# Hybrid mixer of a two-block network: decay spread from a split, block ends in one product, another order at its end

## The reference, cut to what matters

```python
dt = softplus(dt_raw + dt_bias);  a = -exp(a_log);  adt = dt * a
acs = cumsum(adt within chunks of 128)                     # per head
lmat = exp(where(tri, acs[l] - acs[s], -inf))              # decay between two tokens
y_diag = einsum((cc . bc) * lmat, xc)
states = einsum(bc, exp(acs[end] - acs), xc);  chunk_decay = exp(acs[end])
y_off = einsum(cc, prev_state, exp(acs))
y = y_diag + y_off + d_skip * xs
yg = rmsnorm(y * silu(z), over each of 2 groups of 256) * ssd_norm_w
out = concatenate([attn_out, yg]) @ w_out
```

## Time and profile before

| | |
|---|---|
| median of 3 runs | 3323.21 us (3322.04 to 3326.91) |
| the profiled execution | 3323.83 us, its span 3322.1 us |
| PE busy | 3273.5 us, 99% of the span, 15372 instructions |
| DVE, ACT, POOL busy | 55%, 35%, 2% |
| mean granted clock | 0.992 |
| first hybrid mixer, heads 3 to the output product | 2204 to 2300 us of the span |
| second hybrid mixer, the same part | 2818 to 2914 us |

### The profile page before, as it was taken

How to read it: one execution, slowest core, us unless ns; L and a number is a source line. 1 busy time by engine, 2 the same in 40 slices (tenths; PEclk the granted TensorE clock), 3 DMA queues, 4 the chain that set the end, 5 groups by cost and what they waited for, 6 DMA issues and landing times.

```text
span 3322.1 us, 37176 instructions
## 1 busy us (share of the span) xinstructions
PE 3273.5 (99%) x15372; PEld 2709.9 (82%) x15372; DVE 1818.9 (55%) x2599; ACT 1163.1 (35%) x1617; POOL 74.7 (2%) x108
## 2 busy tenths in 40 slices
PE   8999999999999999999999999999999999999999
PEld 6888876888888888887788888887788888878887
DVE  5664366666436664357566635876533368563332
ACT  5222253332233222263322223654322245442221
POOL 1000000000000000000000000100000010000000
PEclk8999999999999999999999999999999999999999
DMA  5443321344333443332244433210223222022322
GB/s 155 142 148 119 101 84 51 127 140 150 114 110 115 139 140 120 97 100 64 89 140 141 135 106 103 80 51 30 98 89 98 95 87 87 1 89 90 101 95 70
DMA packets 334238, 339.86 MB, mean 102 GB/s; under 512 B 12406, under 2 KB 329112, under 8 KB 334072
## 3 DMA queue, kind: packets, MB, share of 16 engines
q1 hardware_dynamic: 332112, 333.80, 30.9%
q0 software_dynamic: 1728, 3.62, 0.4%
q10 hardware_dynamic: 232, 0.06, 0.0%
HBM read 335.36 MB, written 2.10 MB: 102 GB/s over the span
## 4 chain that ended last, share of the span: by engine, by line
PE 90%; DVE 6%; ACT 2%; issue 1%; DMA 0%; SPq 0%; DVEq 0%; ACTq 0%
PE ps L135 88%; PE ps L138 2%; DVE ar L100 1%; DVE wl L100 1%; DVE ar L108 1%; ACT wh L95 1%; ACT ar L95 1%; DVE hl L108 0%; DVE T L108 0%; DMA raw<-in_ffn_w 0%; ACT L95 0%; ACT ch L95 0%; DVE ar L117 0%; ACT hh L95 0%; DVE T L100 0%
## 5 line engine op out<-in xcount | busy, mean ns | idle before, releaser
L135 PE MATMUL ps<-hh,wl 128*128 128x512 f32 x2760 | 1088.7, 394 | 13.9 <-DVE hl L108 9.4
L100 DVE TENSOR_TENSOR wl<-raw,wh 128x1024 fp32r<-128x1024 f32 (+2 forms) x547 | 654.0, 1197 | 774.4 <-ACT wh L95 774.0
L135 PE MATMUL ps<-hh,wh 128*128 128x512 f32 x2760 | 1076.8, 390 | 0.0
L135 PE MATMUL ps<-hl,wh 128*128 128x512 f32 x2760 | 1076.8, 390 | 0.0
L95 ACT ACTIVATE wh<-raw 128x1024 fp32r<-128x1024 f32 (+2 forms) x547 | 560.6, 1027 | 466.2 <-PE ps L135 461.3
L135 PEld LDWEIGHTS ps<-hh,wl 128*128 128x128 f32 x2760 | 520.0, 188 | 128.1 <-issue 18.6
L135 PEld LDWEIGHTS ps<-hh,wh 128*128 128x128 f32 x2760 | 519.6, 188 | 108.9
L135 PEld LDWEIGHTS ps<-hl,wh 128*128 128x128 f32 x2760 | 520.2, 188 | 104.4 <-issue 0.6
L135 PE MATMUL ps<-uh,wl 128*128 128x512 f32 x1056 | 412.0, 390 | 0.0
L135 PE MATMUL ps<-uh,wh 128*128 128x512 f32 x1056 | 411.2, 389 | 0.0
L135 PE MATMUL ps<-ul,wh 128*128 128x512 f32 x1056 | 411.1, 389 | 0.0
(11 more groups left out here) (241 smaller groups left out, 2722.3 us busy)
## 6 DMA issues: line engine op xcount, KB each, us to landing
raw<-in_ffn_w SPq DMA_DIRECT2D x120, 1024.0 KB, 5.1
raw<-in_w_ada SPq DMA_DIRECT2D x48, 1024.0 KB, 5.2
raw<-in_w_gate_up SPq DMA_DIRECT2D x44, 1024.0 KB, 5.0
raw<-in_m_w_in SPq DMA_DIRECT2D x26, 1024.0 KB, 5.6
raw<-in_w_down SPq DMA_DIRECT2D x16, 1024.0 KB, 5.2
raw<-in_ffn_w SPq DMA_DIRECT2D x16, 768.0 KB, 4.3
raw<-in_w_in SPq DMA_DIRECT2D x12, 1024.0 KB, 5.3
raw<-in_m_w_out SPq DMA_DIRECT2D x8, 1024.0 KB, 5.2
```

Source lines behind the costliest of these rows:

```text
L100: return self.issue(lambda e: e.tensor_tensor(out, a, b, op))
L135: return self.issue(lambda e: e.matmul(out, l, r, start=start, stop=stop, skip_group_check=True))
```

## The change

- `ad` (8 rows at partitions 32 to 39) is split: ACT writes `adh`, DVE `adl`, in free parts of `hl`, in the first step of `states()`. The spreads in `weigh` and the product with `X3` contract over these 8 rows, one-pass, with `adl` and then `adh`. `X3` is written as fp32r after that. POOL no longer clears `ad` and `X3`.
- DVE writes the chunk ends, masked by head, into 32 columns (`ends`); one product of 8 rows and 32 columns takes the place of the eight.
- The squares of slice 0 are added to those of slice 1 on DVE (`y01`); `frame_means(0)` is gone.
- `weigh(2)` moves into the step of `frames(1)`, and everything behind it comes one step earlier: frames 2 in head 7, frames 3 and means 2 in head 8, means 3 in head 9 and, in head 9's second slot, the wait for `v8` and `along`, ahead of `values(7)`.
- DVE forms `v8` in three operations instead of two.
- The output product of tiles 0 and 1 runs over slices 0, 4, 1, 5, 2, 6, 3, 7 in one go; ACT's and DVE's parts of attention's and of the recurrence's slices follow in turn, with DVE's `scaled` between them.

```diff
@@ -205,7 +205,8 @@
         sq = [sb(f"sq{i}", [128, S])[0] for i in range(2)]
         acc, _ = sb("acc", [128, S])
         T1 = [sb(f"T1{i}", [128, S])[0] for i in range(2)]
-        T3 = [sb(f"T3{i}", [128, S])[0] for i in range(2)]
+        X3, o_3 = sb("X3", [128, S], F32R)
+        T3 = [sb("T30", [128, S], F32, o_3)[0], sb("T31", [128, S])[0]]
         adab, _ = sb("ada", [128, 424])
         mod, _ = sb("mod", [128, 96])
...
@@ -1081,8 +1074,8 @@
                     W = [d.rearrange(tok4, b=4) for d in xd]
                     Bt = [sp[:, 8, :], sp[:, 9, :]]
                     PV = [None, sp[:, 10, :], sp[:, 11, :], sp[:, 12, :]]
-                    X3 = T3[0][:, :]
                     E2 = [T3[1][:, :], sp[:, 13, :]]
+                    adh, adl = hl[32:40, 6, :], hl[32:40, 7, :]
                     b = banks.take((s, "dtk"))
                     pe.wait_ge(worked, (s, "ad"))
                     for a, src in enumerate((sq[1], ad)):
...
@@ -1091,10 +1084,8 @@
                             done = pe.tr(b[:, c:c + 8], src[32:40, 128 * k:128 * k + 128], ident[32:40, 32:40])
                     done.then_inc(formed, (s, "dtk"))
                     b = banks.take((s, "ends"))
-                    ends = ad.rearrange("p (b n) -> p b n", n=128)[:, :, 127]
-                    for hd in range(8):
-                        done = pe.mm(b[:, 4 * hd:4 * hd + 4], ident[:, 32 + hd:33 + hd].to_broadcast([128, 128]), ends)
-                    done.then_inc(formed, (s, "ends"))
+                    pe.wait_ge(worked, (s, "ends"))
+                    pe.mm(b[:, 0:32], one[32:40, :].to_broadcast([8, 128]), sq[0][32:40, 0:32]).then_inc(formed, (s, "ends"))
 
                     def turned(t):
                         b = banks.take((s, "xt", t))
...
@@ -1113,14 +1104,20 @@
                         done.then_inc(formed, (s, "sn", c))
 
                     def weigh(t):
+                        pe.wait_ge(hi_part, (s, "ad"))
+                        pe.wait_ge(lo_part, (s, "ad"))
                         for hd in (2 * t, 2 * t + 1):
                             b = banks.take((s, "w", hd))
-                            pe.mm(b[:, :], ident[:, 32 + hd:33 + hd].to_broadcast([128, 128]), ad, True, False)
+                            row = identr[32:40, 32 + hd:33 + hd].to_broadcast([8, 128])
+                            pe.mm(b[:, :], row, adl, True, False)
+                            pe.mm(b[:, :], row, adh, False, False)
                             pe.mm(b[:, :].rearrange(tok4, b=4), above[:, :], identr[:, :].unsqueeze(1).to_broadcast([128, 4, 128]),
                                   False, True).then_inc(formed, (s, "w", hd))
                         b = banks.take((s, "e", t))
                         pe.wait_ge(worked, (s, "X3"))
-                        pe.mm(b[:, :], X3[:, 128 * t:128 * t + 128], ad).then_inc(formed, (s, "e", t))
+                        rows = X3[32:40, 128 * t:128 * t + 128]
+                        pe.mm(b[:, :], rows, adl, True, False)
+                        pe.mm(b[:, :], rows, adh, False, True).then_inc(formed, (s, "e", t))
 
                     def frames(t):
                         b = banks.take((s, "y2", t))
...
@@ -1138,7 +1135,6 @@
                         done.then_inc(formed, (s, "y", t))
 
                     def frame_means(t):
-                        pe.wait_ge(squared, (s, "y", t))
                         for k in range(4):
                             done = pe.mm(bs[:, 4 * t + k:4 * t + k + 1], E2[t % 2][:, 128 * k:128 * k + 128], ones[:, 0:1])
                         done.then_inc(formed, (s, "ys", t))
...
@@ -1166,22 +1162,23 @@
                     frames(0)
                     yield 1
                     frames(1)
-                    yield 1
+                    weigh(2)
+                    yield 1
+                    weigh(3)
                     bs = banks.take((s, "ystat"), hold=True)
-                    frame_means(0)
-                    weigh(2)
-                    yield 1
+                    pe.wait_ge(worked, (s, "y01"))
                     frame_means(1)
-                    weigh(3)
                     yield 1
                     frames(2)
                     yield 1
                     frames(3)
                     yield 1
+                    pe.wait_ge(squared, (s, "y", 2))
                     frame_means(2)
+                    yield 1
+                    pe.wait_ge(squared, (s, "y", 3))
                     frame_means(3)
                     banks.drop((s, "ystat"))
-                    yield 1
                     yield 1
                     pe.wait_ge(pooled, (s, "v8"))
                     for g in range(2):
...
@@ -1211,16 +1208,16 @@
                     between()
                     if hd > 1:
                         values(hd - 2)
+                while next(ssd, 0):
+                    pass
                 for j in range(4):
                     b = banks.take((s, "cat", j), freed=(lo_part, (s, "c", j)))
                     pe.wait_ge(*left_of((s, "val", 7)))
                     for q in range(4):
                         done = pe.tr(b[:, 128 * q:128 * q + 128], A(12 + q)[:, 128 * j:128 * j + 128], ident[:, :])
                     done.then_inc(formed, (s, "cat", j))
-                rest = begin(s, [("out", 0), ("out", 1)], ch, cl, (s, "c"), (0, 1, 2, 3))
-                while next(ssd, 0):
-                    pass
-                out_product(s, nxt, rest)
+                begin(s, [("out", 0), ("out", 1)], ch, cl, (s, "c"), (0, 4, 1, 5, 2, 6, 3, 7))
+                out_product(s, nxt, False)
 
             def constants():
                 b = banks.take("vt12")
...
@@ -1831,13 +1828,16 @@
                                 w.then_inc(*((curved, (s, "we", hd, c)) if c < 3 else (left(key), key)))
                         act.wait_ge(formed, (s, "e", t))
                         if t > 1:
-                            act.wait_ge(formed, (s, "ys", t - 2))
+                            act.wait_ge(*((formed, (s, "ys", 1)) if t == 3 else (worked, (s, "y01"))))
                         act.f(E2[t % 2], ps((s, "e", t))[:, :], ACT.Exp, scale=-1.0).then_inc(left((s, "e", t)), (s, "e", t))
 
                     def frames(t):
                         act.wait_ge(worked, (s, "yg", t))
                         act.f(E2[t % 2], A(16 + t), ACT.Square).then_inc(squared, (s, "y", t))
 
+                    act.wait_ge(worked, (s, "ad"))
+                    act.wait_ge(used, G_of[(s, "z", 3)])
+                    act.f(hl[32:40, 6, :], A(43)[32:40, :], ACT.Copy).then_inc(hi_part, (s, "ad"))
                     act.wait_ge(worked, (s, "de"))
                     act.f(cd, al, ACT.Exp, scale=-1.0).then_inc(curved, (s, "cd"))
                     act.f(de, de, ACT.Exp).then_inc(curved, (s, "de"))
...
@@ -1863,12 +1862,6 @@
                     yield 1
                     frames(3)
                     yield 1
-                    yield 1
-                    yield 1
-                    for g in range(2):
-                        for t in (2 * g, 2 * g + 1):
-                            act.wait_ge(*((worked, (s, "yn", t)) if t % 2 == 0 else left_of((s, "al", g))))
-                            part((s, "c", 4 + t), A(16 + t), ch[:, 4 + t, :])
 
                 ssd = states()
...
@@ -1901,12 +1894,14 @@
                     if 0 < hd < 9:
                         turn(hd - 1)
                     between()
+                while next(ssd, 0):
+                    pass
                 for j in range(4):
                     act.wait_ge(formed, (s, "cat", j))
                     part((s, "c", j), ps((s, "cat", j))[:, :], ch[:, j, :])
+                    act.wait_ge(*(left_of((s, "al", j // 2)) if j % 2 else (worked, (s, "yn", j))))
+                    part((s, "c", 4 + j), A(16 + j), ch[:, 4 + j, :])
                 begin(s, [("out", 0), ("out", 1)])
-                while next(ssd, 0):
-                    pass
                 out_product(s, nxt, True)
 
             def constants():
...
@@ -2772,7 +2767,7 @@
                            m[:, 4:8].unsqueeze(2).to_broadcast([128, 4, 64]), MUL).then_inc(left(key), key)
 
                 def states():
-                    X3, als = T3[0][:, :], T1[0][:, 64:160]
+                    als = T1[0][:, 64:160]
                     al = als[:, 0:32].rearrange("p (b h) -> p b h", b=4)
                     cd = als[:, 32:64].rearrange("p (b h) -> p b h", b=4)
                     de = als[:, 64:96].rearrange("p (b h) -> p b h", b=4)
...
@@ -2832,14 +2827,15 @@
                         dve.wait_ge(curved, (s, "z"))
                         dve.tt(y, y, A(24 + t), MUL).then_inc(worked, (s, "yg", t))
 
-                    dve.wait_ge(pooled, (s, "X3"))
-                    shares(X3, 64).then_inc(worked, (s, "X3"))
                     dve.wait_ge(formed, (s, "dtk"))
                     dve.copy(T1[0][:, 0:64], ps((s, "dtk"))[:, 0:64]).then_inc(left((s, "dtk")), (s, "dtk"))
```

(84 more changed lines are left out.)

3 lines of the change are left out of this document (1 added, 2 removed).

## The result

The changed kernel takes 3337.2 us (median of 6 executions, 3333.9 to 3338.5) against 3324.1 for the kernel before in the same runs (the 3323.2 above is the first three of them): the ratio is 1.0037, 95% interval 1.0027 to 1.0047. It is 13 us slower, where 14 us less were forecast. The two profiled executions differ by as much (span 3336.4 against 3322.1).

What follows compares the result with a forecast made beforehand. TensorE, busy 99% of the span, was taken as the bound; per mixer -5.0 + 0.4 - 0.9 + 0.95 - 2.45 = -7.0 us, -14.0 in two, from 3323.2 to about 3310 us, range 3304 to 3318.

Steps and rivals of the forecast that it cites:

- the price of a product with 8 rows: Decay spreads in `weigh` and with `X3`: split spreads take 0.45 us instead of 0.87, gaining 5.0 us a mixer.
- as much as the f32 form: Dearer bound on the split decay spreads: 8-row one-pass products cost what the f32 form does, so no gain.
- the clock in the heads' loop: Heads 5 to 7: the forecast counted no half clock there; rows showing 0.50 outside the end would prove it wrong.
- Rival D: Heads 5 to 7: 8-row products uphold the clock less; half clock through three turns gives 3369 us; 4%.
- the wait of 0.4 us that was charged in head 7: Turn of head 7: PE waits 0.3 to 0.4 us following PSUM banks; charged 0.4 us a mixer, bounds 0 and 2.5.
- The first stretch: Before head 4's scores: block ends save PE 1.7 us, but waits and the split's chain make it lose 0.95 us.
- rival A: Mixer end: half clock lasts through `along`, `values(7)` and transposes; both mixers 3315 us, one 3312; 27% together.
- The end: Mixer end: `cl` waits go, a GpSimd wait comes, the clock returns before `values(7)`; gain 2.45 us a mixer.
- C: Heads' loop becomes bound by ACT and DVE behind it, `weigh` giving back half its gain; 3314 us, 14%.
- E: Spreads: one-pass products with few rows cost as the f32 form, first stretch loses 2.5; 3322 us, 5%.
- The rule on transposes: Skill's rule that transposes don't count for the clock gate; by it, end transposes couldn't help the clock, giving rival A's time.

Runs made afterwards that it cites:

- the run with 64 rows: The changed kernel with its spreads contracting over 64 rows (partitions 0 to 63, all but eight zero) instead of 8: 3319.1 us, ratio 0.9988 to the kernel before.
- The kernel before with 8 rows: The kernel before with its f32 spreads contracting over the 8 filled rows instead of 128, nothing else: 3368.4 us, ratio 1.0133.
- With 128 rows: The changed kernel with split, one-pass decay spreads over all 128 partitions, zero beside the 8 rows: 3313.5 us, ratio 0.9965 to the kernel before.
- 32: The changed kernel with 32 rows (partitions 32 to 63, all but eight zero) in the spreads instead of 8: 3336.1 us, ratio 1.0036 to the kernel before.
- the old spreads: The changed kernel with the spreads of the kernel before (f32, 128 rows, no split), all else of the change: 3317.9 us, ratio 0.9986 to the kernel before.
- the later split: The 128-row variant of the changed kernel, with ACT's high part and `X3` one step later and DVE's low part after `decayed(3)`: 3313.1 us, ratio 0.9965.
- the run with the block ends alone: The kernel before with the block ends in one product and nothing else: 3324.2 us, ratio 0.9998.
- the chain of the split costs 1.0 (measured alone): The kernel before with one-pass split spreads over 128 rows, split made in the first step, nothing else: 3316.5 us, ratio 0.9975.

## Why the prediction was wrong

- **The step that failed first: the price of a product with 8 rows.** "I take the full one-pass price, because the small transposes from 8 rows show no extra cost beside their neighbours." Those transposes stand in a row of their own kind and have 8 columns, so they say nothing of a product of 512 columns beside one of 128 rows. Measured: 1.09 us a head instead of 0.68, and a slot of 2.84 us instead of 1.84. The gain of 5.0 us was 0.8 (four slots, 0.2 each). The bound "as much as the f32 form" was close to the truth. By the run with 64 rows this step is 4.1 us a mixer of the error.
- **The step that failed second, and weighs more: the clock in the heads' loop.** The sum kept it at 1.00 and has no term for it. Measured: 20.5 us a mixer at 0.50 (17.1 in heads 5 and 6, 3.4 in head 7), beside the end's 6.8. By the run with 64 rows that is 9.5 us of the error.
- **Rival D was right on the clock**, at 4%. Its mechanism and place are what the runs show (8 rows uphold the clock less, heads 5 to 7), and more than its 14 us at half clock came. Its extent, three whole turns and 3369 us, was too large for this kernel. Its price alone does not give the measured time either: half of 20.5 us less the 7.0 makes 3330; it is the dearer steps, which D did not have, that bring it to 3337. The kernel before with 8 rows, at 3368.4, is near D's number by both costs together, which says nothing for D's sum. What spoke against D, "attention's products in between are dense", was too weak: they did bring the clock back, at 2253.7 us, 0.4 us ahead of the first product of `frames` (2254.05), but only after 10.4 us of them at half clock:

```profile
2254.05 0.83 PE L135 MATMUL ps<-ar,sp 128*128 128x128 f32 x6
```

- **The sum with the rows put right is near the forecast's sum.** With 128 rows the loop gave -4.7 us (forecast -4.6) and the whole 3313.5 us against 3310. The agreement in the loop is partly luck: the slot is 1.94 us, not 1.84 (0.4 us less gain a mixer), while the wait of 0.4 us that was charged in head 7 is not in the list of PE's waits. In the profiled execution (3315.2 us) the first mixer gained 4.4 us and the second 6.6, where 7.0 were forecast. The first stretch costs 1.2 and 1.6 us instead of 0.95, and the first mixer's end has the clock at half for 13.7 us, as rival A has it (26.6 us from the last column products to tile 2, 24.1 in the second mixer). Two falls of 3.4 us at 2331 and 2700 us, outside the part that was changed and not in the traces of before and after, cost up to 1.7 us each; no run shows what brings them about. The half clock at the end differs between the traces that keep the change's order there: 6.8 us in both mixers with 8, 32 and 64 rows, 13.7 and 6.8 with 128, 13.7 in both with the old spreads, 3.4 and 13.7 with the later split. One trace a kernel does not say which is the rule.
- **The first stretch** was right in mechanism: the 1.7 us of the `ends` products are eaten by waits, that for ACT first (1.1 us; measured alone the block ends gain nothing, 3324.2), and the chain of the split costs 1.0 (measured alone). It was mis-sized by 0.4 us: 1.35 instead of 0.95.
- **The end** was right in its terms within 0.3 us: 2.3 us of wait for GpSimd (2.6), `along` at half clock 3.6 us (3.4), `values(7)` 2.9 (2.6), from the transposes to the output product 2.8 (2.95), no wait for `cl`. The sum was -2.45, measured -2.5. The clock came back 1.1 us into `values(7)`, not ahead of it.
- **Rivals C and E**: the list of PE's waits has none for ACT in heads 5 to 7, so C is out. E named nearly the right price of a one-pass product with few rows, but no fall of the clock.
- **The rule on transposes** that was weighed: in the changed kernel the clock came back before the `cat` transposes and stayed at 1.00 through their 1.94 us, and from 2210 to 2212 us it was 1.00 before. These stretches are short. More telling is the second mixer of the run with the block ends alone: the clock fell behind the idle time among the transposes, which could speak for the rule, and came back 4.5 us into a stretch of nothing but transposes, which speaks against the Trainium skill's rule as it is written (TensorE: Matmul & The Clock Gate, section "Part 4: PE-mode transpose").

On the covered loads, the Trainium skill (TensorE: Matmul & The Clock Gate, section "Part 3: Packing small matmuls — row/col tiling", "The mechanism") says in its list of what overlaps that weight loads overlap with products in flight only when the row group differs; its first paragraph also lets a load go ahead when it targets the background weight buffer. The rows here do not agree with the "only": loads of 128 rows behind products of 128 rows start 0.23 us ahead of their product, those behind a product of 8, 32 or 64 rows do not. They fit the first paragraph for 128 behind 128.

## What to carry to other kernels

Do not cut the contraction of a product down to the rows that hold data when it stands among products of 128 rows: here, with zeros in the other rows, a one-pass spread took no more time, its weights loaded under cover, and the clock stayed up. Price a new form of product from a row where it stands beside the same neighbours; if there is none, give the dearer bound a real share of the chances, and ask of the clock too whether any row shows it with such products. Work removed from PE counts only as far as the bank that the next product needs is empty, and a short chain through GpSimd should lie beside PE's longest independent work, not ahead of it.

## What the runs showed of the hardware that was not expected

- The rows that a product contracts over count for the granted clock, whatever they hold. With the same instructions and columns in the spreads, heads 5 and 6 had 0.50 with 8 rows for 17 us and with 32 rows for 10 to 17 us, and 1.00 with 64 and 128. Whether the number of rows or their place decides is not shown.
- A change between products of 8, 32 or 64 rows and of 128 rows costs some 0.2 us each way (1.09 instead of 0.70 us for a head with two changes; in f32, with 8 rows, 1.48 instead of 1.10), the same for the three numbers of rows.
- The largest loss was with 8 rows in f32 in the old order: 41 us at half clock in heads 5 to 8 of the first mixer and 34 in the second, 44 us of time in all. Form and order are not told apart there.
- Transposes behind an idle gap of 1.09 us went on at 0.50 for 3.4 us in one mixer of three traces and came back to 1.00 with nothing but transposes in between (2826.2 to 2829.6 us in the run with the block ends alone).
